# A two-block transformer on one core: last row, norm and first group by halves of the tokens

## What is computed

```python
def first_block(x, ...):
    h = rms_norm(x, ffn1_pre_g[l])
    x = x + 0.5 * rms_norm(swiglu(h, ffn1_w_in[l], ffn1_w_out[l]), ffn1_post_g[l])
    h = rms_norm(x, mix_pre_g[l])
...
    x = x + rms_norm(mixed, mix_post_g[l])
    h = rms_norm(x, ffn2_pre_g[l])
    x = x + 0.5 * rms_norm(swiglu(h, ffn2_w_in[l], ffn2_w_out[l]), ffn2_post_g[l])

def second_block(x, ...):
    for l in range(DEPTH_2):
        x = layer_norm(ALPHA * x + 0.5 * swiglu_2(x, ffn1_gate[l], ffn1_up[l], ffn1_down[l]), ln_g[l, 0], ln_b[l, 0])
        h = x @ w_in[l]
...
        x = layer_norm(ALPHA * x + mix, ln_g[l, 1], ln_b[l, 1])
        x = layer_norm(ALPHA * x + 0.5 * swiglu_2(x, ffn2_gate[l], ffn2_up[l], ffn2_down[l]), ln_g[l, 2], ln_b[l, 2])
```

## Time and profile before

| | us |
|---|---|
| median of 3 runs | 3035.84 |
| lowest, highest | 3031.92, 3036.48 |
| the profiled execution | 3040.53 |
| its span | 3038.7 |
| TensorE busy | 2953.3 (97%) |
| VectorE busy | 1327.3 (44%) |
| ScalarE busy | 1002.3 (33%) |
| GpSimd busy | 403.4 (13%) |

### The profile page before, as it was taken

The page is one execution under the profiler, slowest core; times in us unless marked ns, Lnnn a source line. Parts: engine busy times, 40 slices in busy tenths (PEclk is TensorE's granted clock), DMA queues, the critical chain, the costliest instruction groups (busy, mean ns, idle before and its releaser), DMA issues.

```text
span 3038.7 us, 32142 instructions
## 1 busy us (share of the span) xinstructions
PE 2953.3 (97%) x13432; PEld 2434.2 (80%) x13432; DVE 1327.3 (44%) x1783; ACT 1002.3 (33%) x1345; POOL 403.4 (13%) x427
## 2 busy tenths in 40 slices
PE   8999989899999999999999999999999999899998
PEld 6888876577888788888887888888888788788887
DVE  5553267645343433334655333343333465543333
ACT  4232234453232333223333332233222333342222
POOL 3110057312110000011231000100001123200010
PEclk9999989899999999999998999999999899899998
DMA  4333212122233232232212222222333221122222
GB/s 137 96 97 97 97 56 69 17 72 88 97 97 97 85 97 97 97 96 77 77 49 64 97 97 97 97 77 97 97 97 96 72 76 49 63 97 97 96 91 77
DMA packets 76016, 260.39 MB, mean 86 GB/s; under 512 B 11728, under 2 KB 11856, under 8 KB 75856
## 3 DMA queue, kind: packets, MB, share of 16 engines
q1 hardware_dynamic: 75872, 258.34, 26.4%
HBM read 255.03 MB, written 2.10 MB: 85 GB/s over the span
## 4 chain that ended last, share of the span: by engine, by line
PE 93%; DVE 4%; issue 1%; ACT 1%; POOL 0%; DMA 0%; SPq 0%; DVEq 0%; POOLq 0%; ACTq 0%
PE bank L325 25%; PE bank L327 25%; PE bank L326 25%; PE bank L339 2%; PE bank L340 2%; PE bank L345 2%; PE bank L436 2%; PE bank L683 2%; PE bank L446 1%; DVE Hl L1291 1%; PE bank L374 1%; PE bank L375 1%; PE bank L378 1%; PE bank L590 1%; PE bank L608 1%
## 5 line engine op out<-in xcount | busy, mean ns | idle before, releaser
L1283 DVE TENSOR_TENSOR wlo<-wraw,whi 128x1024 fp32r<-128x1024 f32 x474 | 588.1, 1253 | 832.4 <-ACT whi L792 831.7
L325 PE MATMUL bank<-Hh,whi 128*128 128x512 f32 x2320 | 911.5, 393 | 11.0 <-DVE wlo L1283 9.1
L326 PE MATMUL bank<-Hh,wlo 128*128 128x512 f32 x2320 | 906.5, 391 | 0.0
L327 PE MATMUL bank<-Hl,whi 128*128 128x512 f32 x2320 | 906.1, 391 | 0.0
L792 ACT ACTIVATE whi<-wraw 128x1024 fp32r<-128x1024 f32 x479 | 498.9, 1055 | 957.8 <-DMA wraw<-weights 957.5
L325 PEld LDWEIGHTS bank<-Hh,whi 128*128 128x128 f32 x2320 | 438.3, 189 | 106.4 <-issue 11.7
L327 PEld LDWEIGHTS bank<-Hl,whi 128*128 128x128 f32 x2320 | 437.8, 189 | 92.4
L326 PEld LDWEIGHTS bank<-Hh,wlo 128*128 128x128 f32 x2320 | 437.9, 189 | 89.3
L325 PE MATMUL bank<-Ah,whi 128*128 128x512 f32 x1056 | 411.8, 390 | 0.0
L326 PE MATMUL bank<-Ah,wlo 128*128 128x512 f32 x1056 | 410.9, 389 | 0.0
L327 PE MATMUL bank<-Al,whi 128*128 128x512 f32 x1056 | 410.8, 389 | 0.0
(11 more groups left out here) (258 smaller groups left out, 2528.1 us busy)
## 6 DMA issues: line engine op xcount, KB each, us to landing
wraw<-weights SPq DMA_DIRECT2D x479, 512.0 KB, 3.4
X<-x_t SPq DMA_DIRECT2D x8, 256.0 KB, 6.9
y_t<-X SPq DMA_DIRECT2D x8, 256.0 KB, 2.0
Y<-masks SPq DMA_DIRECT2D x1, 512.0 KB, 8.5
MUb<-ssm SPq DMA_DIRECT2D x1, 256.0 KB, 7.9
tmp<-ssm SPq DMA_DIRECT2D x1, 256.0 KB, 3.9
zsum<-attention SPq DMA_DIRECT2D x1, 256.0 KB, 4.0
MUb<-attention SPq DMA_DIRECT2D x1, 256.0 KB, 4.2
```

The costliest lines, as they stand in the source:

```text
L325: pe.matmul(b, sh, mh, start=start, stop=False)
L326: pe.matmul(b, sl, mh, start=False, stop=False)
L327: signal(pe.matmul(b, sh, ml, start=False, stop=stop), keys)
L1283: dve.tensor_tensor(wlo[:, u % NS, :], wraw[:, u % NS, :], f32(whi[:, u % NS, :]), SUB).then_inc(*S.done("weights_lo", ("lo", u)))
```

## The change

The last output row of every stage but f1 is done by halves of the 256 first and 256 last tokens (HALF), with the weight tiles of its last 16 tiles (8 in a mixer) kept in their buffers for both halves. Second halves go to a bank of their own. The statistics of the first half are taken while TensorE works on the second half of the row, those of the second half inside the next stage's first group. That group (gemm_halves) takes its rows in two passes of four k; within a pass all four k for the first half, then for the second, with the 16 tiles kept. VectorE and ScalarE norm, write Hh, X and Hl by halves in the order first half of rows 0 to 3, second half of 0 to 3, first half of 4 to 7, second half of 4 to 7. In an RMS seam the scaled row goes to tmp in SBUF, not back into the bank. In f2 the group's results are put aside (raw4) and the input norm's sums move into the second group. Four empty tiles are added to each h stage's stream, so that every stage starts on a unit's boundary, and GpSimd makes wlo of two units per seam. Everything is still computed.

```diff
+HALF = T // 2
...
         plan.extend((f"pool{g}_{l}", 0, 0) for g in range(4))
+        plan.extend((None, 0, 0) for _ in range(4))
         halves(f"out_{l}")
...
-    pool_lo = {START[s] // 8 + AHEAD for s in ("m1", "f2", "a0", "h0", "b0", "a1", "h1", "b1") if START[s] % 8 == 0}
+    pool_lo = {START[s] // 8 + AHEAD for s in ("m1", "f2", "a0", "h0", "b0", "a1", "h1", "b1")}
+    pool_lo |= {START[s] // 8 + 3 for s in ("f2", "a0", "h0", "b0", "a1", "h1", "b1")}
...
+        def gemm_halves(use, fresh, keys, beside):
...
+            for k0 in (0, 4):
+                tiles = []
+                for h in range(2):
+                    hs = halves[h]
+                    for k in range(k0, k0 + 4):
+                        if not h:
+                            tiles.extend(tile() for _ in range(4))
+                        pe.wait_ge(*S.at(("Hh", fresh, k, h)))
+                        for i in range(4):
+                            hi, lo, ends = tiles[4 * (k - k0) + i]
...
+                            pe.matmul(bs[i][:, hs], hi, Hh[:, k, hs], start=k == 0 and h == 0, stop=False,
+                                      skip_group_check=True)
+                            pe.matmul(bs[i][:, hs], lo, Hh[:, k, hs], start=False, stop=False, skip_group_check=True)
+                        pe.wait_ge(*S.at(("Hl", fresh, k, h)))
...
+                            signal(pe.matmul(bs[i][:, hs], hi, Hl[:, k, hs], start=False, stop=k == KD - 1,
+                                             skip_group_check=True),
...
+                        beside(h, k)
...
+        def last_row(st, nk, mh, ml, sums, beside, keys=()):
+
+            late = min(nk, 16)
+            b = open_bank((st, "row", 7), True)
+            for k in range(nk - late):
+                hi, lo, ends = tile()
+                mm3(b[:, :], hi, lo, mh[:, k, :], ml[:, k, :], k == 0, False, ends)
+            if nk > late:
+                sums()
+            tiles = [tile() for _ in range(late)]
+            for i in range(late):
...
+                mm3(b[:, 0:HALF], hi, lo, mh[:, k, 0:HALF], ml[:, k, 0:HALF], k == 0, i == late - 1,
+                    (("row a", st),) if i == late - 1 else ())
+            B.let_go((st, "row", 7))
+            if nk == late:
+                sums()
+            b = open_bank((st, "row b"), True)
+            for i in range(late):
...
+                mm3(b[:, 0:HALF], hi, lo, mh[:, k, HALF:T], ml[:, k, HALF:T], i == 0, i == late - 1,
+                    ends + ((("full", (st, "row", 7)),) + keys if i == late - 1 else ()))
+                beside(i)
...
+            def beside(i):
+                if i == 2:
+                    stats(0)
+                if i == (9 if nk > KD else 7):
+                    scale(0)
...
+            def next_beside(h, k):
+                if not h and k == 0:
+                    stats(1)
+                if not h and k == 2:
+                    scale(1)
...
+            stats(0)
+            scale(0)
+            dve.wait_ge(*S.at(("full", (st, "stats", 0))))
+            dve.wait_ge(*S.at(("sq", st, 0)))
+            row(0, 0)
...
+            row(1, 0)
+            rest(0, 0)
+            stats(1)
+            row(2, 0)
+            rest(1, 0)
+            scale(1)
+            row(3, 0)
+            rest(2, 0)
+            rest(3, 0)
...
+            def row(k, h):
+                hs, t = halves[h], tmp[k % 2]
+                b = bank((st, "stats", h))
...
+                dve.tensor_tensor(t[:, hs], Y[:, k, hs], b[:, 0:HALF], MUL).then_inc(
...
+                dve.scalar_tensor_tensor(X[:, k, hs], t[:, hs], post_g(k), X[:, k, hs], MUL, ADD).then_inc(
...
+        def lo_first(st):
+
+            lo(START[st] // 8 + 2)
+            lo(START[st] // 8 + 3)
...
+        for k0, h in ((0, 0), (4, 0), (0, 1), (4, 1)):
+            for k in range(k0, k0 + 4):
+                sp.wait_ge(*S.at(("X", "b1", k, h)))
+                sp.dma_start(out_d[:, k, halves[h]], X[:, k, halves[h]]).then_inc(stored, 16)
```

More of the change, by code:

```diff
@@ L41 @@
 MIX2 = 5 * 4 * KD
-MIX2_OUT = 4 + KD * KD
+MIX2_OUT = 8 + KD * KD
 START = {}
@@ new lines, in out_ln, with square_7, root @@
+            hi_to(ends[KD - 1] - 1)
+            table(ACT.Sqrt)
+            def square_7(h):
+                act.wait_ge(*S.at(("Y7", st, h)))
+                act.activation(sq[:, halves[h]], Y[:, 7, halves[h]], ACT.Square).then_inc(
+                    *S.done("squares", ("sq", st, h)))
+            def root(h):
+                o = 2 * h
+                act.wait_ge(*S.at(("variance", st, h)))
+                act.activation(small[:, 12 + o:14 + o], small[:, 8 + o:10 + o], ACT.Sqrt, bias=epsc[:, 1:2]).then_inc(
+                    *S.done("roots", ("root", st, h)))
@@ L1453, in out_ln @@
-            dve.wait_ge(*S.at(("sq", st)))
-            for k in range(EARLY + last):
-                centred(k)
-            dve.wait_ge(*S.at(("full", (st, "scale"))))
-            for k in range(KD):
-                if k >= EARLY + last:
-                    centred(k)
-                dve.wait_ge(*S.at(("mean off", st, k)))
-                dve.tensor_tensor(Y[:, k, :], Y[:, k, :], b2[:, :], MUL).then_inc(
-                    *S.done("rows", ("normed", st, k), empties=[(st, "scale")] if k == KD - 1 else []))
-                if k and not last:
-                    dve.wait_ge(*S.at(("X", st, k - 1)))
-                    split_lo(then, k - 1, X[:, k - 1, :])
@@ new lines, in rest @@
+            def rest(k, h):
+                if not last:
+                    dve.wait_ge(*S.at(("X", st, k, h)))
+                    split_half(then, k, h)
+            dve.wait_ge(*S.at(("row a", st)))
+            dve.wait_ge(*S.at(("X shifted", st, 7)))
+            r, part = bank((st, "row", 7)), nk > KD
+            dve.scalar_tensor_tensor(Y[:, 7, 0:HALF], r[:, 0:HALF], half, X[:, 7, 0:HALF], MUL, ADD).then_inc(
+                *S.done("rows", ("Y7", st, 0), empties=[] if part else [(st, "row", 7)]))
@@ new lines, in out_ln @@
+            dve.scalar_tensor_tensor(Y[:, 7, HALF:T], bank((st, "row b"))[:, 0:HALF], half,
+                                     (Y if part else X)[:, 7, HALF:T], MUL, ADD).then_inc(
+                *S.done("rows", ("Y7", st, 1), ("Y", st, 7), empties=[(st, "row b")]))
+            row(1, 0)
+            rest(0, 0)
+            stats(1)
+            row(2, 0)
+            rest(1, 0)
+            scale(1)
+            row(3, 0)
+            rest(2, 0)
+            rest(3, 0)
+            order = ((4, 0), (0, 1), (4, 1)) if last else ((0, 1), (4, 0), (4, 1))
@@ L1470, in then_ @@
+            for k0, h in order:
+                if (k0, h) == (0, 1):
+                    dve.wait_ge(*S.at(("full", (st, "stats", 1))))
+                    dve.wait_ge(*S.at(("sq", st, 1)))
+                for k in range(k0, k0 + 4):
+                    row(k, h)
+                    if k > k0:
+                        rest(k - 1, h)
+                rest(k0 + 3, h)
         def then_(ins, *keys):
```

535 lines of the change are left out of this document (382 added, 153 removed).

## The result

| | before | after |
|---|---|---|
| median | 3035.54 (20 runs, 3031.22 to 3042.13) | 3041.02 (20 runs, 3035.59 to 3045.85) |
| ratio to before | | 1.0017, 95% interval 1.0011 to 1.0023 |
| the profiled execution, its span | 3040.53, 3038.7 | 3037.16, 3035.4 |
| mean granted clock in it | 0.970 | 0.984 |

The account below looks back on a forecast made before the run. TensorE holds 93% of the 3038.7 us span, so only its waits and slow running at seams can be won. Seam gains and losses sum to 8.2, less 4 for the clock: 4 us faster, median about 3032; range 3008 to 3050.

Parts of the forecast that it names:

- pace of a half: TensorE's 256-column matmuls: 120 ns each where half of 227 is 113, costing 13 us in all.
- a0 to h0, b0 to a1, a1 to h1: LN seams with 22-tile rows: 47.6 us each with halves, against 51.3, 51.4 and 54.6; gains 3.7, 3.8 and 7.0.
- output rows of h0; of h1: Padding puts h0's output rows on a unit boundary, so they take h1's 57.8 instead of 51.2: a loss of 6.6.
- m1o to f2 with the moved sums: RMS seam: VectorE's residues and adds wait for GpSimd; 45.3 against 38.4 without the moved sums, a loss of 6.9.
- f2 to a0: RMS seam where only two weight splits meet residues and adds: 46.9 against 45.7, a loss of 1.2.
- the end: From the last row's start to the kernel's end, 37 us before: halves gain 0.4.
- clock: TensorE's clock falls at half of five LN seams, 1.6 us each: a loss of 4 us.
- The LN seams with 8 tiles: h0o to b0 and h1o to b1: 38.6 us with halves against 44.1 and 41.2, gains 5.4 and 2.6.
- Rival 3: The clock falls at all seven seams and is slow to return, 2.4 us each, 17 instead of 4: 3045; chance 12%.
- the lock in the RMS seam: VectorE operations with two SBUF inputs and GpSimd ones reading SBUF exclude each other; without it the sum is 8 us better.
- the stall that goes at a1 to h1: A 4-column VectorE operation took 4.04 us while GpSimd cleared Sc; after the change the clearing misses the small operations.
- the 3 us wait in h0's rows: In h0's output rows TensorE waits some 3 us for a weight split, as in h1's before.

Follow-up runs that it names:

- ln8_whole: The changed kernel with the seams h0o to b0 and h1o to b1 back to whole rows, against the kernel before: 3036.3 us, ratio 0.9996.
- pad_early_centre: Kernel before plus padding, earlier split of the sixth output row's unit and VectorE's mean subtractions first, no halves: 3026.6 us, ratio 0.9976 to the kernel before.
- best_centre: Changed kernel plus RMS add from PSUM, earlier split of the sixth output row's unit, VectorE's mean subtractions first: 3028.5 us, ratio 0.9980 to the kernel before.
- pad_only: The kernel before with only the four empty tiles in each h stage (and one more GpSimd split at three seams): 3032.6 us, ratio 0.9983.

## Why the prediction failed

The sum's terms beside the traces (positive is faster; where profiles of the same work differ, the mean of them, with h's output rows and seams from five profiles with the padding and halves, and two of before):

| term | forecast | measured |
|---|---|---|
| pace of a half | 120 ns | 120 ns |
| a0 to h0, b0 to a1, a1 to h1 | 3.7, 3.8, 7.0 | 2.6, 2.7, 5.9 |
| h0, h1 up to the head norm; b0, a1 behind their first group | 0 | -1.7; -0.8 |
| h0o to b0, h1o to b1 | 5.4, 2.6 | together -0.8 |
| output rows of h0; of h1 | -6.6; 0 | -3.7; +1.4 |
| m1o to f2 with the moved sums | -6.9 | -6.8 |
| f2 to a0 | -1.2 | +0.2 (46.17 after; 45.70 and 46.96 before) |
| the end (b1 from its second group on) | +0.4 | +0.5 (last row to the end +0.9, rows before it -0.4) |
| clock | -4 | in the rows above |
| sum | 4 | -0.5 |

**The step that failed** is "The LN seams with 8 tiles", 38.6 us and gains of 5.4 and 2.6, together with the term "Clock", 1.6 us at half of five LN seams. The two gains, 8.0, came out at -0.8:

- Where the clock stays up the halved form takes 39.8, not 38.6: 2.4 us for the two seams.
- It stayed up in only two of ten passes (five profiles), which took 39.8 to 45.2, on average 42.5. Falls cost 2.7 a pass, 5.4 for the two seams, where the clock term had 0.8 a pass.
- The whole form took 42.1 on average in the two profiles of before (4 passes), less than the first profile alone: 1.1.

A fall costs by its length: 1.5, 3.1 and 5.4 us where TensorE's clock was at 1.2 GHz for 3.4, 10.2 and 17.1 us of the stretch (that time is twice what PEclk lacks to 1, times the stretch). The term's 1.6 fits only the shortest. Whole rows pay no less for it: 40.0 with 10.2 us at 1.2 GHz (ln8_whole), 41.2 to 41.7 with 13.7, and with 17.1 us 44.1 in the first profile of before (with a further wait of 0.99) and 42.8 in pad_early_centre, whose row is:

```profile
1636.39:1679.15 42.76, 40.24 (x174) 33.89 (x172) 25.15 (x41) 22.10 (x28) 4.29 (x3) 0.80 0.19 62
```

So with the clock alike (42.9 beside 40.0, 45.2 beside 42.8) the halved seam is 2.4 to 2.9 us longer than the whole one; by the price of a half, 240 of them are 1.6 of it. That ate up what halves won there by the clock, 0.91 on average in the ten passes beside 0.83 in the four of before. Of the eight passes with a fall, it began in five at 6.3 to 6.6 us into the stretch, at the small sums of Y and its square, and in three at 11.3, at the end of a wait of 1.65 for the first Hh. ln8_whole shows the loss alone, best_centre that it outlives the wait ahead of it.

The argument for a fall was made at a 22-tile seam, and there (a0 to h0, b0 to a1, a1 to h1) the halved form had three in 30 passes (ten profiles), each worth 1.0 us and begun within 0.7 us of the end of the 0.98 us wait. Rival 3 (the clock falls and is slow to come back, 3045) had the mechanism and nearly the size, but not the place: it had all seven seams.

The second miss is smaller: 1.1 us at each 22-tile seam, and 2.5 behind the seams that I had at nothing. In the seam b0 to a1 matmuls that had to wait start 0.2 instead of 0.12 ahead of the next one, and there are further waits of 0.1 to 0.55 for VectorE and ScalarE; what makes the 2.5 was not taken apart.

**Right** were the half's price, the order and cause of the waits, the lock in the RMS seam and its 7 us (with the split between seam and next group off by 1.2 each way), the stall that goes at a1 to h1, and the 3 us wait in h0's rows. For that stall, the gain belongs to the padding (pad_only), and perhaps part of h0o to b0 too, which had 41.3 with the padding alone; the forecast counted both to the halves.

**What stays open.** The terms give 0.5 us slower, the medians 5.5 and 8. The profiled executions of the changed kernel (3037.2 and 3041.0) lie 3.8 and 3.3 under the medians of their runs, those of before (3040.5 and 3038.2) 5.0 and 5.3 over theirs, and the mean clocks say the same: 0.984 and 0.983 in the profiles after beside medians of 0.983 and 0.981, 0.969 in the second profile of before beside 0.972 to 0.973. So the traces flatter the change. Where the timed runs lose or win the clock is argued only: in the stretches that varied. What makes the clock fall at the head of a halved 8-tile row in one execution and not in the next was not found either.

## What to carry to other kernels

Price an edit at each place where it is applied: the same edit won 2 to 3 us at long rows, nothing at m1o to f2 and lost at short rows, and only the sum was measured at first. A raised mean clock (0.971 to 0.982) is no gain by itself when the work grew with it (1968 halves, 13 us by their price). When an operand moves from PSUM to SBUF, look at what GpSimd does at that moment; keeping it in a free half of a bank gave 8 us in the two RMS seams.

## What the hardware showed that was not expected

- With the same instructions and waits, the granted clock in the h stages differed from execution to execution: 39.8, 42.9 and 45.2 us for one seam. The halved 22-tile LN seams were 48.7 in 27 of 30 passes, 49.7 in the other three.
- A fall can begin well behind the wait: at h1o to b1 of the changed kernel it began at 2635.5, 13 us after the last wait of over 1 us (to 2622.3) and 1.5 after two column sums of 0.9 each, and lasted 17 us.
- The add with one operand in PSUM was 484 ns beside GpSimd's sums of squares, the residue with two in SBUF 722, in the same 37 us.
